# The triangular substitution of a chunked delta rule, started two weight panels earlier, and two small turns moved inside the next panel

## The reference

```python
kb = kc * bc[..., None]
A = jnp.where(strict, jnp.einsum("bnhid,bnhjd->bnhij", kb, kc) * gamma, 0.0)
eye = jnp.eye(C, dtype=jnp.float32)
T = lax.linalg.triangular_solve(A + eye, jnp.broadcast_to(eye, A.shape),
                                left_side=True, lower=True)
u = jnp.einsum("bnhij,bnhje->bnhie", T, vc * bc[..., None])
w = jnp.einsum("bnhij,bnhjd->bnhid", T, kb * eG)
```

## Time and profile before

| | us |
|---|---|
| median of three runs | 2238.38 |
| lowest, highest | 2235.93, 2238.72 |
| the profiled execution | 2238.95 |
| its span, first to last instruction | 2237.1 |
| PE busy | 2199.4 (98%) |
| DVE busy | 1279.9 (57%) |
| ACT busy | 923.6 (41%) |
| POOL busy | 482.8 (22%) |

### The profile page before, as it was taken

The page is one execution under the profiler, slowest core; times in us unless marked ns, Lnnn a source line. Parts: engine busy times, 40 slices in busy tenths (PEclk is TensorE's granted clock), DMA queues, the critical chain, the costliest instruction groups (busy, mean ns, idle before and its releaser), DMA issues.

```text
span 2237.1 us, 27579 instructions
## 1 busy us (share of the span) xinstructions
PE 2199.4 (98%) x10414; PEld 1805.9 (81%) x10414; DVE 1279.9 (57%) x2131; ACT 923.6 (41%) x1643; POOL 482.8 (22%) x363
## 2 busy tenths in 40 slices
PE   8999999999999999999999999999999999999998
PEld 5777898888888888788887888888887778888886
DVE  6768334677486684857886444334666764333333
ACT  5777433436422221245675322222445553222223
POOL 1000431242311010153662110101232321101012
PEclk9999999999999999999999999999999999999998
DMA  5241211232323333232112333332321122323322
GB/s 188 67 122 58 86 57 56 67 95 62 99 87 102 94 94 94 92 97 85 57 57 66 99 94 96 102 95 87 92 87 57 45 67 89 100 94 100 98 92 87
DMA packets 69012, 193.94 MB, mean 87 GB/s; under 512 B 14608, under 2 KB 18960, under 8 KB 68880
## 3 DMA queue, kind: packets, MB, share of 16 engines
q1 hardware_dynamic: 67584, 189.82, 27.5%
q10 hardware_dynamic: 1296, 2.36, 0.4%
HBM read 185.34 MB, written 6.82 MB: 86 GB/s over the span
## 4 chain that ended last, share of the span: by engine, by line
PE 85%; DVE 5%; ACT 3%; issue 3%; POOL 1%; DVEq 1%; DMA 1%; POOLq 0%; SPq 0%; ACTq 0%
PE bank L316 16%; PE bank L318 16%; PE bank L317 16%; PE bank L352 7%; PE bank L354 7%; PE bank L353 7%; PE bank L1780 2%; PE bank L1110 1%; DVE b_arena L533 1%; DVE b_arena L1943 1%; PE bank L1492 1%; PE bank L724 1%; ACT b_arena L1860 1%; PE bank L1806 1%; PE bank L1807 1%
## 5 line engine op out<-in xcount | busy, mean ns | idle before, releaser
L247 ACT ACTIVATE b_wh<-b_raw 128x1024 fp32r<-128x1024 f32 (+2 forms) x344 | 354.2, 1030 | 1042.7 <-PE bank L318 781.0
L316 PE MATMUL bank<-b_xh,b_wh 128*128 128x512 f32 x1080 | 421.3, 390 | 0.4 <-DVE b_wl L252 0.3
L318 PE MATMUL bank<-b_xh,b_wl 128*128 128x512 f32 x1080 | 420.6, 389 | 0.0
L317 PE MATMUL bank<-b_xl,b_wh 128*128 128x512 f32 x1080 | 420.5, 389 | 0.0
L252 DVE TENSOR_TENSOR b_wl<-b_raw,b_wh 128x1024 fp32r<-128x1024 f32 (+1 forms) x296 | 360.3, 1217 | 105.0 <-ACT b_wh L247 103.6
L352 PE MATMUL bank<-b_xh,b_wh 128*128 128x512 f32 x744 | 310.0, 417 | 1.5 <-DVE b_wl L252 0.9
L592 POOL TENSOR_TENSOR b_yl<-b_arena,b_yh 128x512 fp32r<-128x512 f32 x66 | 112.0, 1697 | 873.7 <-ACT b_yh L570 873.7
L354 PE MATMUL bank<-b_xh,b_wl 128*128 128x512 f32 x744 | 292.5, 393 | 0.0
L353 PE MATMUL bank<-b_xl,b_wh 128*128 128x512 f32 x744 | 291.0, 391 | 0.0
L316 PEld LDWEIGHTS bank<-b_xh,b_wh 128*128 128x128 f32 x1080 | 202.7, 188 | 44.8 <-issue 1.2
L318 PEld LDWEIGHTS bank<-b_xh,b_wl 128*128 128x128 f32 x1080 | 202.7, 188 | 42.6
(11 more groups left out here) (412 smaller groups left out, 3277.8 us busy)
## 6 DMA issues: line engine op xcount, KB each, us to landing
b_raw<-in_zga SPq DMA_DIRECT2D x16, 512.0 KB, 3.5
b_raw<-in_c0up SPq DMA_DIRECT2D x16, 512.0 KB, 3.5
b_raw<-in_c1up SPq DMA_DIRECT2D x16, 512.0 KB, 3.5
b_raw<-in_fqk SPq DMA_DIRECT2D x16, 512.0 KB, 3.5
b_raw<-in_s0up SPq DMA_DIRECT2D x16, 512.0 KB, 3.5
b_raw<-in_s1up SPq DMA_DIRECT2D x16, 512.0 KB, 3.5
b_raw<-in_m0up SPq DMA_DIRECT2D x16, 512.0 KB, 3.5
b_raw<-in_m1up SPq DMA_DIRECT2D x16, 512.0 KB, 3.5
```

The source lines that it names most:

```text
L247: act.activation(wh[:, par, cols], raw[:, par, cols], ACT.Copy).then_inc(w_hi, 1)
L316: pe.matmul(bank[:, :], wh[:, par, w], hi[:, x, :], start=(k == 0), stop=False)
L317: pe.matmul(bank[:, :], wh[:, par, w], lo[:, x, :], start=False, stop=False)
L318: last = pe.matmul(bank[:, :], wl[:, par, w], hi[:, x, :], start=False, stop=(k == kt - 1))
```

## The change

The table `SOLVE` begins at panel 18 instead of 20. The steps per panel were 4, 4, 3, 3, 3, 6, 8 for panels 20 to 26; they are 2, 3, 3, 3, 3, 3, 3, 5, 6 for panels 18 to 26. SP's part is moved with it: A goes out after the loads of panels 16 and 18 (before: 18 and 20), the blocks come in after the load of 19 (21), the inverse goes out after the load of 29 (30), and the tiles of T come in after the load of 30 (31). Because tiles of q are still being turned at panel 18, the scratch of ACT's squares no longer shares its place with the solve's product. The turn of tile 5 moves from behind panel 9 to behind slice 1 of panel 10, the turn of tile 6 from slice 3 to slice 4, and the turn of the k coefficients from behind panel 11 to behind slice 5 of panel 12. ACT's and DVE's parts of these steps keep their places.

```diff
-        prod32, junk, qscale = yb[:, 4, :], [yb[:, 5, :], yb[:, 4, :]], [yb[:, 6 + s, :] for s in range(2)]
+        prod32, junk, qscale = yb[:, 4, :], [yb[:, 5, :], yb[:, 7, :]], [yb[:, 6 + s, :] for s in range(2)]
-        SOLVE = {20: (0, 4), 21: (4, 8), 22: (8, 11), 23: (11, 14), 24: (14, 17), 25: (17, 23), 26: (23, 31)}
+        SOLVE = {18: (0, 2), 19: (2, 5), 20: (5, 8), 21: (8, 11), 22: (11, 14), 23: (14, 17), 24: (17, 20), 25: (20, 25), 26: (25, 31)}
-                if n in (18, 20):
-                    for hd in range(4 * (n == 20), 4 + 4 * (n == 20)):
+                if n in (16, 18):
+                    for hd in range(4 * (n == 18), 4 + 4 * (n == 18)):
-                if n == 21:
+                if n == 19:
                     sp.wait_ge(d_a, 16 * GH)
-                if n == 30:
+                if n == 29:
                     sp.wait_ge(g_w, 1)
-                if n == 31:
+                if n == 30:
                     sp.wait_ge(d_w, 16 * NB)
-        TURN = {5: [0], 6: [1], 7: [2], 8: [3], 9: [4, 5], 10: [7]}
+        TURN = {5: [0], 6: [1], 7: [2], 8: [3], 9: [4], 10: [7]}
+            def rows_turned(r):
+                pe.wait_ge(g_c, 1 + r)
+                for b in range(NB):
+                    t = pe.transpose(pb[6][0:8, B(b)], cc[:, r, GH * b:GH * b + GH], ident)
+                t.then_inc(g_cr, 1)
-                    if m == 10 and k == 3:
+                    if m == 10 and k == 1:
+                        turn(5)
+                    if m == 10 and k == 4:
                         turn(6)
+                    if m == 12 and k == 5:
+                        rows_turned(0)
-                if m in (11, 19):
-                    pe.wait_ge(g_c, 1 + (m == 19))
-                    for b in range(NB):
-                        t = pe.transpose(pb[6][0:8, B(b)], cc[:, int(m == 19), GH * b:GH * b + GH], ident)
-                    t.then_inc(g_cr, 1)
+                if m == 19:
+                    rows_turned(1)
-                for c in ([6] if m == 10 else []) + TURN.get(m, [m - 3] if 11 <= m < 27 else []):
+                for c in {9: [4, 5], 10: [6, 7]}.get(m, TURN.get(m, [m - 3] if 11 <= m < 27 else [])):
-                    if m == 20:
+                    if m == 18:
                         dve.wait_ge(d_u, 16 * NB)
```

## The result

| | median us | lowest, highest | executions |
|---|---|---|---|
| before | 2236.26 | 2234.31, 2238.72 | 10 |
| changed | 2241.88 | 2241.39, 2244.03 | 10 |

The ratio is 1.0022 (95% interval 1.0014 to 1.0031): slower, by about as much as the 0.2% that the prediction took as its bound. By this ratio the change costs 4.9 us; the two medians lie 5.6 us apart. Neither profiled execution is a typical one. That of the kernel before, 2238.95 us, was slower than every one of its ten runs, and that of the changed kernel, 2241.39 us, was the fastest of its ten.

A forecast was written before the change was run, and what follows sets the result against it. PE, busy for 98% of the span, was taken as the bound. The terms -2.5 + 1.7 + 1.4 + 1.7 = +2.3 on the profiled 2238.95 gave 2241.2, less 0.57 for the median: 2240.7 us, range 2235.0 to 2243.0.

The forecast's parts named there:

- within 0.2%: Whole kernel: time tells no difference from before, between 2233.9 and 2242.9 us; chance 0.82.
- Turns of tiles 5 and 6: PE's turns around panel 10: the wait before turn 6 shrinks from 0.80 to 0.11 us, gain 0.69 us.
- The coefficients: Panel 12: the 2.2 us wait becomes one of 2.3 us at the rows' first use, which comes 2.5 us earlier.
- The clock behind it: PE after the new wait for the rows: the clock falls again as before, costing 1.7 us, bounds 0 and 1.7.
- The solve and the transfers: Panels 18 to 31: T's 1.5 us wait goes; panel 31 lands late, L1110 loses 1.4 us, plus 1.7 us slow clock.
- The sum: Whole kernel: -2.5 + 1.7 + 1.4 + 1.7 = +2.3 us on the profiled execution's 2238.95 us.
- only one wait, or none, would slow the clock: PE behind the two new waits: one slow stretch gives 2239.0 us, neither gives 2237.3; chance 0.27.
- panel 31 would not be late: End of the solve: panel 31's load lands in 3.9 us, before ACT wants it; 2237.2 us, chance 0.15.
- all three waits would go: PE's waits: all vanish and nothing replaces them, -6.2 us, 2232.2 us; chance 0.06.
- the slower case: Panel 31's load lands later than 235.2; from 2.2 us more the sum passes +4.5, about 2243.5 us; chance 0.07.

The follow-up runs named there:

- Turns only: Kernel before with only the turns of tiles 5 and 6 and of the coefficients moved; solve and SP's order as before: ratio to before 1.0006.
- the turn put back: Changed kernel with the coefficients' turn back behind panel 11, all else staying changed: ratio to before 1.0016.
- the rows' halves made early: Changed kernel with the coefficients' turn behind slice 3 of panel 12 and the rows' halves copied earlier on ACT and DVE: ratio to before 0.9998.
- SP's order undone: Changed kernel with SP writing the inverse behind panel 30's load and reading T behind panel 31's, as before; early solve kept: ratio to before 1.0003.
- the waits filled: Changed kernel with unused matmuls added, 8 ahead of the wait for the rows and 12 ahead of the first pair's: ratio to before 0.9999.
- solve and SP's order alone: Kernel before with only the early solve and SP's moved order; all PE turns where they stood: ratio to before 1.0018.
- the rows early with SP's order undone: Changed kernel with the rows' halves copied earlier and SP's order around the inverse and T as before the change: ratio to before 0.9985.

## Why the prediction was right

Its time, 2240.7 us with a range of 2235 to 2243, holds the measured 2241.88. Of its chances the one for "within 0.2%" was far the largest; what was measured stands at 0.22% with an interval that reaches to both sides of that bound. By the traces the mechanism is the one forecast, with one term too small. That the time came out so near is in part luck, as the sum below shows: the change itself was forecast at +2.3 us, and it costs 4.9 by the ratio and 5.6 by the medians.

*Turns of tiles 5 and 6.* Right. 0.69 us was forecast for the turn behind panel 11 and it moved from 87.48 to 86.66, of which 0.17 is the earlier start of the whole trace. ACT's run began 0.72 us earlier, where I took 0.46; 0.17 of that is again the start, and the gap of 0.46 us ahead of it is gone.

*The coefficients.* Right in mechanism and size: no wait at the turn, 2.1 us (2.3 forecast) at the first use, which moved by 2.6 us (2.5). Turns only and the turn put back show no effect of the place on PE that the runs can tell; the rows' halves made early show that ACT's order does.

*The clock behind it.* The term that was mis-sized. I took one stretch of 3.4 us, 1.7 us of time, as in the earlier trace rows. It was 6.8 us long in two of the three traces that have this wait with the turn moved (the changed kernel and the turns alone), and 3.4 in that of SP's order undone. By the changed trace the cost was 0.33 + 2.62 = 2.95 us: panel 29 ended 0.33 us later than before, where the first use had been 2.62 earlier. The trace with the waits filled, which has no low clock there, says the same. From the first use of the rows to the end of panel 29 it takes 134.85 us, SP's order undone 136.38 and the changed kernel 137.95, so the stretch of 3.4 us cost 1.5 and that of 6.8 cost 3.1. Why the same wait was followed now by one length and now by the other stays open.

*The solve and the transfers.* Right. T came without a wait, and behind the rows' wait none appeared up to panel 29, so the extra load on DVE at panels 18 to 20 and the later loads of 19 and 20 cost nothing, as forecast. Panel 31's load took 6.1 us, as forecast; ACT was 1.9 us late instead of 1.8, PE idle for 3.1 instead of 2.9, slow for 3.4 us after it. SP's order undone shows the order of these transfers as the cause; solve and SP's order alone show the price without the turns.

*The sum.* +2.3 us was forecast on the profiled execution and the spans differ by 2.5. That is luck in part. Between the two rows of the table, where all that was changed lies, the changed trace is 3.7 us longer, 1.4 more than forecast, and nearly all of that is the longer slow stretch (+1.25). Outside of them the changed execution was kinder: 0.2 us at the start, and 1.0 in the last low stretch of the program, which the change doesn't touch. The medians differ by more, 5.6 us, because the profile of before was 2.7 us above its median and that of the changed kernel 0.5 below its own. So the forecast was built on an execution that took longer than the usual one. Added to the median of the ten runs, 2236.26, its +2.3 would have given 2238.6, which is 3.3 too low.

*The rivals.* That only one wait, or none, would slow the clock fell by the two stretches at 0.50. That panel 31 would not be late fell by its landing; that all three waits would go, by both new waits. That the load would land much later still, the slower case, fell by the landing at 235.6. Measured against before, though, the change cost more than the 4.5 us that the prediction took as its bound for slower: 4.9 us by the ratio, 5.6 by the medians.

*What stays open.* The runs of before spread over 4.4 us and those of the changed kernel over 2.6. The traces show two things that differ from execution to execution with no edit near them. Among the nine kernels that are alike up to the first row of the table, that row comes at 59.89 us in one trace and at 61.88 in another; ACT's first copy of x already waits for its DMA until 5.7 us in one (turns only) and until 6.8 in another (changed). And behind the sums of squares at 984 us the clock fell for 3.4 us in two traces of ten, SP's order undone and the rows' halves early, which cost them 1.6 us. The same stretch in the first of these and in before:

```profile
985.20:988.60 3.40, 3.40 (x10) 2.62 (x9) 1.04 (x5) 0.00 (x0) 2.16 (x3) 0.50 0.00 0
...
986.60:990.00 3.40, 3.40 (x16) 2.80 (x15) 1.10 (x5) 0.00 (x0) 2.18 (x3) 1.00 0.00 0
```

Whether some runs of before lack the slow stretch behind the 2.2 us wait, no trace shows. The three traces with that wait (before, solve and SP's order only, the turn put back) all have it, but only one of them is of before, and that execution was slower than all ten runs.

## What to carry to other kernels

A wait names who came last, and that engine has an order of its own: before moving the waiting instruction, follow the result that it leads to through the other engines' queues, since a wait whose source is bound elsewhere turns up again at the next use. A transfer that is started early takes its place in the DMA queue from the one behind it (panel 31's load: 3.9 us ahead of the four reads, 6.1 behind them); ask which of the two is wanted first. A wait of PE of 2.1 us or more cost here its length and the slow work behind it, so where such a wait can't be removed, work of no use put into it can still win time. And where a change is worth a few microseconds, one trace is too little to build the forecast on: compare the profiled time with the median first, and take differences between two rows that enclose the change.

## What was not expected of the hardware

- The low clock behind the 2.1 us wait for the rows lasted 6.8 us in two traces and 3.4 in a third, with the same instructions behind it; behind all other waits of 2.1 to 3.7 us it lasted 3.4 us.
- Between 60 and 250 us, waits of 1.4 and 1.5 us were not followed by a low clock in the three traces that have one (before, SP's order undone, the rows early with SP's order undone); waits of 2.1 to 3.7 us were in all. A long wait is not needed for it, though: at 984 us the clock fell in two traces of ten behind 0.5 us of idle time and sixteen matmuls of 128x1.
- Matmuls of no use in the waits kept the clock up and were worth 5.1 us.
- Seven loads of a panel that went out right behind the four reads of T took 5.9 to 6.9 us to land, one in each of seven traces; the load ahead of the reads took 3.8 to 4.1 in all ten. In the three kernels with SP's order undone and the solve early, the next load goes out 2.0 us after the reads and took 3.7 to 4.4. PE's wait at the first pair follows the landing of panel 31: 3.1, 3.5, 3.6 and 3.7 us with 6.1, 6.4, 6.5 and 6.6.
